# Choice of experts beside the second half's z products, and row units of the second half's merge and routing spread anew

## The reference, cut to what matters

```
u = rmsnorm(h) ; z, xs, bs, cs, dt, sb, sc, sx, gates = split(u @ w_in)
xbc = silu(causal_dwconv([xs, bs, cs])) ; y = scan(xs, bs, cs, dt)
y_ssd = group_rmsnorm(y * silu(z)) @ ssd_w_out
h = h + (sigmoid(g0) * y_ssd + sigmoid(g1) * y_sc) @ w_o
x = rmsnorm(h) ; q = x @ w_q                      # 8 heads, 2 halves of 128
s = q . sub_keys ; sv, si = top_k(s, 16)          # "search"
cs, ci = top_k(sums of pairs of sv, 16)           # "choice"
eidx = i1 * 128 + i2 ; g = softmax(cs)
act = gelu(x . expert_u[eidx])                    # "dots": 128 rows a token
h = h + sum_k (g * act)_k * expert_v[eidx_k]      # "adds": 128 rows a token
```

## Time and profile before

| | |
|---|---|
| median of 3 runs | 2902.28 us (2900.76 to 2905.21) |
| the profiled execution, whole | 2909.61 us |
| its span in the trace | 2907.9 us |
| PE busy | 2373.7 us (82%) |
| DVE busy | 1769.6 us (61%) |
| POOL busy | 1196.5 us (41%) |
| ACT busy | 546.9 us (19%) |
| gathers (software queue) | 536.94 MB, 47.6% of the 16 engines' span |
| other loads (hardware queue) | 293.33 MB, 25.3% |

### The profile page before, as it was taken

How to read it: one execution, slowest core, us unless ns; L and a number is a source line. 1 busy time by engine, 2 the same in 40 slices (tenths; PEclk the granted TensorE clock), 3 DMA queues, 4 the chain that set the end, 5 groups by cost and what they waited for, 6 DMA issues and landing times. The chain is left out here.

```text
span 2907.9 us, 28130 instructions
## 1 busy us (share of the span) xinstructions
PE 2373.7 (82%) x9836; PEld 1673.8 (58%) x9836; DVE 1769.6 (61%) x3599; ACT 546.9 (19%) x1475; POOL 1196.5 (41%) x1058
## 2 busy tenths in 40 slices
PE   6997989990888887998789694387567999978888
PEld 5855878680773555886464382145455555537666
DVE  2304511158998998486379778989776777711400
ACT  3412210020331221000112211120212210012221
POOL 0000000003676678376257766877663766400000
PEclk9997989995999998999999796698778999988789
DMA  4322044334999999999598999999996999905265
GB/s 150 119 113 87 30 159 151 121 127 163 369 414 413 367 400 388 370 414 415 226 341 295 382 413 400 330 374 412 368 412 249 408 417 413 401 35 213 109 257 220
DMA packets 173228, 832.06 MB, mean 286 GB/s; under 512 B 20880, under 2 KB 21136, under 8 KB 156192
## 3 DMA queue, kind: packets, MB, share of 16 engines
q0 software_dynamic: 147456, 536.94, 47.6%
q1 hardware_dynamic: 25632, 293.33, 25.3%
HBM read 828.09 MB, written 2.10 MB: 285 GB/s over the span
## 5 line engine op out<-in xcount | busy, mean ns | idle before, releaser
L1113 POOL DMA_INDIRECT expert_rows<-in_peer_u,chosen x512 | 634.0, 1238 | 1021.2 <-DVE chosen L1646 684.3
L1113 POOL DMA_INDIRECT expert_rows<-in_peer_v,chosen x512 | 559.1, 1092 | 297.0 <-issue 139.7
L1187 DVE SCALAR_TENSOR_TENSOR expert_rows<-expert_rows,u 128x1024 f32<-128x1024 f32 x512 | 607.4, 1223 | 90.3 <-DMA expert_rows<-in_peer_u,chosen 77.0
L615 PE MATMUL product<-uT,in_slab 128*128 128x272 f32 (+1 forms) x1024 | 241.3, 392 | 77.9 <-DMA in_slab<-in_w_in 77.9
L1147 PE MATMUL expert_sum<-expert_rows,expert_diag 128*128 128x512 f32 x564 | 265.0, 615 | 21.7 <-ACT expert_diag L1134 15.3
L1197 DVE SCALAR_TENSOR_TENSOR h<-expert_rows,expert_coef,h 128x1024 f32<-128x1024 f32 x186 | 239.4, 1287 | 30.4 <-DMA expert_rows<-in_peer_v,chosen 27.1
L615 PEld LDWEIGHTS product<-uT,in_slab 128*128 128x128 f32 x1024 | 194.5, 194 | 109.8 <-issue 78.1
L1197 DVE SCALAR_TENSOR_TENSOR u<-expert_rows,expert_coef,u 128x1024 f32<-128x1024 f32 x181 | 233.0, 1287 | 32.5 <-DMA expert_rows<-in_peer_v,chosen 27.7
L2713 PE MATMUL mlp_up<-mlp_xT,mlp_slab 128*128 128x384 f32 (+1 forms) x1024 | 227.2, 385 | 4.1 <-DMA mlp_slab<-in_w_up 3.1
L2704 PE MATMUL mlp_down<-mlp_slab,upT 128*128 128x512 f32 x512 | 222.0, 593 | 0.0
L2713 PEld LDWEIGHTS mlp_up<-mlp_xT,mlp_slab 128*128 128x128 f32 x1024 | 158.1, 195 | 76.3 <-issue 9.2
(11 more groups left out here) (441 smaller groups left out, 3291.5 us busy)
## 6 DMA issues: line engine op xcount, KB each, us to landing
in_slab<-in_w_in SPq DMA_DIRECT2D x39, 2048.0 KB, 10.5
mix_slab<-in_w_in SPq DMA_DIRECT2D x16, 2048.0 KB, 10.5
mlp_slab<-in_w_up SPq DMA_DIRECT2D x16, 2048.0 KB, 9.1
mlp_slab<-in_w_down SPq DMA_DIRECT2D x16, 2048.0 KB, 9.4
mix_slab<-in_ssd_w_out SPq DMA_DIRECT2D x8, 2048.0 KB, 9.8
out_slab<-in_w_out SPq DMA_DIRECT2D x6, 2048.0 KB, 9.1
expert_rows<-in_w_in SPq DMA_DIRECT2D x4, 2048.0 KB, 7.4
mix_slab<-in_sc_w_out SPq DMA_DIRECT2D x4, 2048.0 KB, 9.5
```

What stands on the lines that cost most here:

```text
L615: ins = pe.matmul(bank[n % 4][:, 0:W], slab[s][:, k, c:c + P], uT[:, k, A:A + W], start=k == 0, stop=k == KD - 1)
L1113: pool.indirect_dma_start(out=self.row(n), out_offset=None, in_=self.tables[0 if dot else 1], in_offset=bass.IndirectOffsetOnAxis(ap=picks ...
L1187: dve.scalar_tensor_tensor(self.row(n), self.row(n), 1.0, u, ALU.mult, ALU.mult, accum_out=dot).then_inc(self.rows_used, 1)
```

## The change

Two things are changed.

**Choice of the first half.** DVE leaves the first half's `route` behind the last search, and makes the choice behind its `leave`, into a buffer of its own, `choice`, which is kept (its two parts later serve the second half as `xs` and `cf`). ACT leaves too, does the exponent of tile 0 (`exponents(act, 0)`) and that of tile 1 within the next stage, behind three z tiles. In the second half's `project` the z products come first, then the convolution. SP loads the z slabs first. ACT waits for `choice_made` between z and the convolution, since it then writes into the choice's buffers. DVE takes 12 units ahead of the first convolution tile where it took 3; 31 x 3 = 93 follow, and 23 are left for `use_rest` where 32 were.

**Units.** `PLAN_ONE` gives merge 150 units instead of 128, so the routing has 98 left instead of 120. Inside the merge `BG_MERGE` goes from (36, 6, 6, 8, 4, 4) to (54, 6, 6, 6, 4, 4). In the routing DVE takes `SETS_F` = 16 units ahead of the first search, 4 behind each search as before, and `SETS_M` goes from (8, 8, 6, 6) to (5, 5, 4, 4): with 16 and 64 units gone, 18 are left, and these all fall into the choice of tile 0. PE takes 3 of 8 units from unit 430 on (before: from 384 on) up to 493 (before 455), and 6 of 8 from there: 38 units instead of 69.

The tables:

```diff
-PLAN_ONE = (128, 128, 128, 8)
+PLAN_ONE = (128, 128, 150, 8)
+SETS_S, SETS_Q, SETS_F, SETS_J, SETS_M = 5, 8, 16, 4, (5, 5, 4, 4)
...
-    IN_SCAN, IN_SEARCH, IN_PAIRS, SEARCH = (1, 3, 6), (1, 3, 6), (1, 2, 4, 5, 6, 7), 72
+    IN_SCAN, IN_SEARCH, IN_PAIRS = (1, 3, 6), (1, 3, 6), (1, 2, 4, 5, 6, 7)
+    SEARCH, PAIRS = sum(PLAN_ONE) + SETS_F, sum(PLAN_ONE) + SETS_F + 16 * SETS_J
...
-BG_MERGE = (36, 6, 6, 8, 4, 4)
+BG_MERGE = (54, 6, 6, 6, 4, 4)
...
-SETS_S, SETS_Q, SETS_J, SETS_M = 5, 8, 4, (8, 8, 6, 6)
```

In `project`, on PE, ACT and DVE (`z_tiles` is the old loop over z, moved into a function, and `drain_z` the old one over its copies):

```diff
+            if half:
+                z_tiles()
             for n in range(CONV):
...
+                if n < 4 and half:
+                    pe.wait_ge(z_used, Z_TILES - 3 + n)
...
+            if half:
+                drain_z(0, 3)
+                choice_exp(act, 1)
+                drain_z(3, Z_TILES)
+
+                act.wait_ge(choice_made, 1)
             for n in range(CONV + 3):
...
-                    bg.use(dve, 3)
+                    bg.use(dve, 3 if n else 12)
```

In `route`, on ACT and DVE:

```diff
+            if bg:
+                for m in range(TT):
+                    bg.diagonals(act, SETS_F + 16 * SETS_J + m * sum(SETS_M) + SETS_M[0] + SETS_M[1])
+                    exponents(act, m)
                 bg.diagonals(act, UNITS)
-            leave(act)
+                leave(act)
+            else:
+                leave(act)
+                exponents(act, 0)
...
+            if bg:
+                bg.use(dve, SETS_F)
...
+            if not bg:
+                leave(dve)
+            chain = Chain(dve, choice_step)
             for m in range(TT):
...
-            leave(dve)
-            if bg:
+            if bg:
+                leave(dve)
                 bg.use_rest(dve)
+            else:
+                dve.sem_inc(made, 1)
+    return exponents, made
```

More of the change, by code:

```diff
@@ L391, in _program @@
         tiles_of = lambda x: x.rearrange("p m (a b) -> p (m a) b", b=TOK)
+        second = ExitStack()
+        choice = []
         def block_one(half, buffers, lend, bg, plans):
@@ L430, in block_one @@
                     end_stage()
+            if half == 0:
+                choice.append(second.enter_context(nc.sbuf_tensor("choice", [P, TT * INNER + GROUPS * TOK], F32,
+                                                                  side="right"))[:])
             with ExitStack() as ctx:
@@ L440, in block_one @@
                 plan()
-                route(frame, slab_loader, ident, xT, slab, chosen[half], weight[half],
-                      state, small.count, bg, [f[2] for f in first[1:]], chosen_ready, keys, keys_in)
+                choice.extend(route(
+                    frame, slab_loader, ident, xT, slab, chosen[half], weight[half], state if half else choice[0],
+                    small.count, bg, [f[2] for f in first[1:]], chosen_ready, keys, keys_in))
                 end_stage()
@@ L587, in _ @@
             enter(sp)
+            parts = [(lambda s: w_in[in_slab(O_XS) + s], 8), (lambda s: w_in[in_slab(O_Z) + s], 4)]
+            if half:
+                parts.reverse()
             for s in range(2):
[L589 to L592, removed]
+                sp.dma_start(slab[s][:], parts[0][0](s)).then_inc(landed[s], 16)
+            slab_loader(sp, [s[:] for s in slab], landed, product, 4, parts)
             leave_sync(sp)
@@ L606, in turn_tile, with z_tiles @@
                 ins.then_inc(turn_done, 1)
+            def z_tiles():
+                for s in range(INNER // SLAB):
+                    pe.wait_ge(landed[s % 2], 16 * (z_slab + s // 2 + 1))
+                    for m in range(TT):
+                        n = s * TT + m
+                        if n >= 4:
+                            pe.wait_ge(z_used, n - 3)
+                        at = A + M + m * P
+                        for k in range(KD):
+                            ins = pe.matmul(bank[n % 4][:], uT[:, k, at:at + P], slab[s % 2][:, k, :],
+                                            start=k == 0, stop=k == KD - 1)
+                            if k == KD // 2 - 1:
+                                ins.then_inc(product, 1)
+                        ins.then_inc(product, 1)
+            if half:
+                z_tiles()
             for n in range(CONV):
@@ L629, in _ @@
             ins.then_inc(dt_done, 1)
[L631 to L644, removed]
+            if half == 0:
+                pe.wait_ge(pre_ready, CONV)
+                z_tiles()
             leave(pe)
@@ L686, in _ @@
                     drain(n - 3)
[L687 to L690, removed]
+            if half == 0:
+                drain_z(0, Z_TILES)
             leave(act)
@@ L1473, in route, with exponents @@
             sem(x) for x in ("q_used", "scores_done", "scores_used", "searched"))
-        step, centred, exped = sem("route_step"), sem("route_centred"), sem("route_exped")
+        step = sem("route_step")
+        choice_step, centred, exped, made = (
+            sem("choice_" + x, keep=not bg) for x in ("step", "centred", "exped", "made"))
+        def exponents(act, m):
+            act.wait_ge(centred, m + 1)
+            act.activation(top_, top_, ACT.Exp).then_inc(exped, 1)
         @block.sync
```

93 lines of the change are left out of this document (55 added, 38 removed).

## The result

| | before | changed |
|---|---|---|
| runs of the comparison | 2903.7 us median (2900.8 to 2908.6, 4 runs) | 2877.3 us median (2870.5 to 2883.1, 4 runs) |
| profiled execution | 2909.6 us, span 2907.9 | 2883.1 us, span 2881.3 |
| ratio | | 0.9894, 95% interval 0.9879 to 0.9910 |

The changed kernel is faster, by 26.5 us between medians and profiled spans, by 31 (26 to 35) by the ratio. The forecast was -35 and 2867, with a range from 2856 to 2884. The time lies in the range, 10 us above the forecast, but what follows is not the sum as it was written. Measured a second time, the ratio was 0.9874 (0.9857 to 0.9891), so -37: the same kernel's gain moves by some 6 us, and the two intervals overlap.

A forecast was written before the change was run, and what follows sets the result against it. DMA moves bytes nearly all the time while experts run, so gains come from stretches where DMA or DVE stand still. Terms -22 + 5 + 3 - 17 - 4 = -35 us, from 2902.3 to 2867.3; range 2856 to 2884.

The forecast's parts named there:

- The choice beside z: First half's choice run beside the z products: scan starts earlier, -22 us, bounds -24 and -10.5.
- a restart: PE's start of the z products after idle time: costs 2.9 us on top of z's 57.1.
- (b): Rival at the z products: slabs land late beside the first gathers, first term only -10.5, 2879 us; chance 0.12.
- (d): Rival at the z products: PE runs z at half clock, 114.1 us, so slower, +19, 2921 us; chance 0.03.
- The taps' step: Second half's convolution: the 31 further tiles keep their step of 4.89 us each.
- Merge: 22 more row units in the merge: dots free on DVE, rows come late, +5 us, bounds 0 and +13.
- rival (a): Bytes bind merge and search: merge +13, search start +8, total -22, 2880 us; chance 0.17.
- Norm and start of the search: More adds in the norm and ahead of the first search: +3 us for both, bounds 0 and +8.
- Searches and choices: Second half: searches keep four units each, 0; two choices lose adds, 80.8 to 63.7 us, -17, bounds -13 and -19.
- The stage behind: After the second half's choices: shorter wait for a 0.5 MB load, -4 us, bounds 0 and -6.
- Everything behind follows in the same order: All after the stage behind the choices: no further gain or loss, no term in the sum.

The follow-up runs named there:

- the units alone: Kernel before with the changed kernel's four unit tables and 16 units ahead of the search, choice unmoved; 0.9962 to before, 0.9982 on the slow-issuing chip.
- the choice alone: Changed kernel with the row units' split of before, except the 12 units before the first taps; 0.9912 to before on a chip like the result's.
- experiment 4: Changed kernel with DVE waiting for each second-half row multiply's end before the next; 0.9881 to before, 1.0152 on the slow-issuing chip.
- experiment 1: Changed kernel with the row units' split of before, so the choice beside z by itself; 0.9912 to before, 0.9952 on the slow-issuing chip.

## Why the prediction was right, and where its sum was not

**The choice beside z, -22: right.** -21.2, -22.7 and -23.5 in three traces. Z began at 669.5 and ended at 726.8 (forecast 668.7 and 728.7). It took 57.31 us, against 57.06 before, where the working put 2.9 us for a restart on top. The restart was there, but it was already in the 57.06. The first eight products and the rest of z, before and then in the changed kernel (columns as in the earlier trace rows):

```profile
877.57:882.97 5.40, 5.40 (x8) 2.38 (x9) 5.33 (x10) 1.00 (x2) 3.95 (x4) 0.65 0.98 393
882.97:934.63 51.66, 51.66 (x121) 22.65 (x119) 41.80 (x72) 4.58 (x8) 39.80 (x34) 1.00 1.02 412
```

```profile
669.49:675.13 5.64, 5.64 (x8) 2.39 (x9) 5.36 (x27) 0.31 (x1) 0.00 (x0) 0.62 0.60 256
675.13:726.79 51.66, 51.66 (x122) 22.96 (x121) 50.42 (x125) 8.34 (x11) 25.44 (x20) 1.00 0.78 306
```

Before, too, z had waited (4.96 us), its first eight products took 5.40 us at a granted clock of 0.65, and the rest ran at 1.00, eight in 3.43. In the changed kernel the eight took 5.64 at 0.62. So the low clock at the start cost 2.0 us before and 2.2 now, and the working counted it twice. Rivals (b) and (d) are out. The taps' step grew from 4.89 to (885.82 - 731.94) / 31 = 4.96, 2.2 us in all, where the working had it the same; that and the restart counted twice cancel, which is luck.

**Merge, +5: the sign was right, the size too large.** From the end of the last scaling by `y_scale` (L958, L1001) to the last add the merge took 284.0 us before, 287.0 and 285.1 in two traces of the changed kernel and 286.0 in the units alone: +1 to +3. The +6.3 of the second trace in the account's second row lies in the scan, 191.0 us against 185.8, where nothing was changed. The working also left four of the 22 units out: behind the pieces of `sc_w_out` DVE takes 16 where it took 12; no time shows for them. The mechanism was as told: DVE's wait for PE at the short convolution becomes a wait for rows. DVE's dots and `sc_sx` grouped in the merge, of before and then of the changed kernel:

```profile
L1187 DVE SCALAR_TENSOR_TENSOR expert_rows<-expert_rows,u 128x1024 f32<-128x1024 f32 x128 | 151.8, 1224 | 38.6 <-DMA expert_rows<-in_peer_u,chosen 36.9 <-DVEq L125 0.2
...
L1383 DVE TENSOR_TENSOR sc_sx<-mix_product,sc 128x516 f32<-128x516 f32 x4 | 2.8, 692 | 39.8 <-PE mix_product L1310 39.8
```

```profile
L1231 DVE SCALAR_TENSOR_TENSOR expert_rows<-expert_rows,u 128x1024 f32<-128x1024 f32 x128 | 153.4, 1224 | 60.2 <-DMA expert_rows<-in_peer_u,chosen 57.7 <-DVEq L127 0.2
...
L1427 DVE TENSOR_TENSOR sc_sx<-mix_product,sc 128x516 f32<-128x516 f32 x4 | 2.8, 690 | 4.6 <-PE mix_product L1354 4.6
```

39.8 us of waiting for PE fall to 4.6, and 36.9 of waiting for rows rise to 57.7. The DMA share is 1.02 in the stretches shown from the merge's second part to the search, as rival (a) wants, and yet its +13 and +8 did not come.

**Norm and start of the search, +3: 4.5**, the same in each kernel with the new units and 0 in the one without.

**Searches and choices, -17: exact for the choices.** From 1555.54 to 1635.27 they took 79.7 us, and from 1537.70 to 1600.44 62.7. The searches took 2.8 us less besides, 118.0 to 115.2, which the sum had at 0. The wait for a score ahead of the second search is what went, 2.88 us before and 0.14 now:

```profile
1445.97 0.49 DVE L1566 MAX8 best<-score 128x8 f32<-128x128 f32 x2 [2.88 <-ACT score L1535]
```

**The stage behind, -4: -3.5.**

**What failed is the sentence "Everything behind follows in the same order", a term of 0.** To the out products it was +10.9 and +2.7 in the two traces of the changed kernel, +5.0 in the choice alone and +10.3 in the units alone. Two things are in it. One is systematic: with a full ring DVE needs no pauses, the gathers slow down and nine to eleven fewer go out in 61 us; experiment 4 shows that. From the stage's start to the latents' scaling this is worth some 2 us: the four traces with 29 to 31 gathers there take 143.7 to 146.3 us, and the two with 40 (before, and the choice alone) 142.3 and 142.6. With the waits it takes 133.9. The other moves with the execution: from there to the out products it was 184.6 before, 193.5 and 185.8 in the two traces of the changed kernel, and 189.3 in the choice alone, whose gathers are as fast as before. DVE waits 5.9 us for rows there before, and 12.3, 6.9 and 10.9 in the other three. What moves it stays open. That the time is in the range has luck in it: the upper end stood at 2884 for rivals (a) and (b), neither of which came, and what took up that room was a cost for which the sum had no term.

The Trainium skill bears on the first, in SBUF — State Buffer, section Who interferes with whom: a VectorE instruction with two SBUF inputs contends with GpSimd instructions that read SBUF, but `tensor_tensor`, as it infers, takes only the read interface and descriptor generation needs the write one, so that it doesn't stall DMA. The dot here is a `scalar_tensor_tensor` with two SBUF inputs, and the indirect gather, which reads its row numbers from SBUF, takes 1.99 us beside it and 0.96 with the pause. That agrees with the first half; the second half doesn't carry over to this pair. Through which interface they meet no run here shows.

## What to carry to other kernels

Where a background stream feeds on a ring, a stage that starts with the ring full is not simply earlier: ask what the feeding engine does while the consumer runs at full pace, and put a term for it into the sum. Work spread out of a stage that only DVE binds gives its full DVE time back there (-17 of -17 here), and it costs less than that where it goes under waits that the trace shows (+1 to +3 and +4.5), even where the DMA share then reads 1.02; of the whole, 11 us (7 to 15) were left at the end. A cost read from one start of an engine may already be in the time read from another: look at the clock over the first instructions of both. And a gain of 5 to 10 us in a trace of one execution is no gain yet, when executions of the same kernel differ by 12.

## What the runs showed of the hardware

**The same program can issue late beside gathers.** The kernel of experiment 1 ran on both kinds of chip. The page's row of its MLP products, on the one like the result's and then on the slow-issuing one:

```profile
L2790 PE MATMUL mlp_up<-mlp_xT,mlp_slab 128*128 128x384 f32 (+1 forms) x1024 | 227.4, 384 | 3.8 <-DMA mlp_slab<-in_w_up 3.1
```

```profile
L2790 PE MATMUL mlp_up<-mlp_xT,mlp_slab 128*128 128x384 f32 (+1 forms) x1024 | 243.5, 397 | 107.3 <-issue 85.6
```

Busy times by stretch in that stage, with rows coming in:

```profile
2400.00:2480.00 80.00, 80.00 (x217) 41.04 (x216) 62.15 (x49) 7.10 (x14) 50.83 (x48) 1.00 1.02 415
```

```profile
2420.00:2500.00 80.00, 32.69 (x61) 13.15 (x59) 80.00 (x66) 0.00 (x0) 60.21 (x65) 0.61 1.02 410
```

The same program, the same 410 to 415 GB/s, but PE does 61 products there for 217, at a granted clock of 0.61 for 1.00, and waits for nothing that the profile shows; 65 gathers go out there for 48. In the in products of experiment 4 single products of 0.59 us stand up to 2.8 us apart. Over the whole program the idle times of this kind (0.6 us or more) come to 161 to 241 us for PE in the seven runs on that chip, and to 11 to 14 on the other; for DVE they come to 47 to 57 and to 8 to 10, and in the first half's choice they stretch 28.3 us to 41.1 (experiment 1). What causes it is open, and so is whether it belongs to the chip: number 3 stands in the record for runs of both kinds, the kernel before at 3109 us in one and at 2908 us in the other. The difference decides whether a change is good: with the waits of experiment 4 the kernel is 1.2% faster than before on the one chip and 1.5% slower on the other.

**A DVE pause of 0.12 us halves a GpSimd gather** (1.99 to 0.96 us), as told in experiment 4.
